# Two fused transformer blocks on one core: the opening of the program in another order

## What is computed

```
def rms_norm(x, g):
    y = x32 * lax.rsqrt(jnp.mean(jnp.square(x32), axis=-1, keepdims=True) + RMS_EPS)
    return (y * g.astype(jnp.float32)).astype(x.dtype)

u = rms_norm(h, g_mix[i])
z = u @ w_in[i]
q_a, k_a, v_a, q_b, k_b, v_b, f_b, gate_logits = jnp.split(z, SPLIT_POINTS, axis=-1)
y_a = sliding_window_attention(q_a, k_a, v_a, swa_sinks[i]) @ w_br_swa[i]
y_b = forgetting_attention(q_b, k_b, v_b, f_b + b_forget[i]) @ w_br_fox[i]
mixed = gates[:, :, 0] * y_a + gates[:, :, 1] * y_b
h = h + mixed @ w_mix_out[i]
```

## Time and profile before

| | us |
|---|---|
| median of 3 runs (lowest, highest) | 914.16 (913.61, 914.38) |
| span of the profiled execution | 912.5 |
| PE busy in it | 884.9 (97%) |
| DVE busy | 588.0 (64%) |
| ACT busy | 442.7 (49%) |
| POOL busy | 43.2 (5%) |
| mean DMA rate | 187 GB/s |

### The profile page before, as it was taken

The page is one execution under the profiler, slowest core; times in us unless marked ns, Lnnn a source line. Parts: engine busy times, 40 slices in busy tenths (PEclk is TensorE's granted clock), DMA queues, the critical chain, the costliest instruction groups (busy, mean ns, idle before and its releaser), DMA issues.

```text
span 912.5 us, 11670 instructions
## 1 busy us (share of the span) xinstructions
PE 884.9 (97%) x4071; PEld 712.6 (78%) x4071; DVE 588.0 (64%) x866; ACT 442.7 (49%) x694; POOL 43.2 (5%) x60
## 2 busy tenths in 40 slices
PE   6999999999999999999799999999999899999996
PEld 6787677787888888887687786778888778888885
DVE  4755544677777777788666795546667654654655
ACT  6545543446555555557553444444534443443442
POOL 1000000011000000020000000001000000000000
PEclk9999999999999999999899999999999899999999
DMA  9853332476999898751374445344545356565551
GB/s 290 285 174 116 93 93 79 136 274 225 353 329 326 321 319 328 246 162 37 120 226 145 156 147 188 93 139 152 176 157 184 108 172 192 161 217 187 165 157 47
DMA packets 87623, 170.43 MB, mean 187 GB/s; under 512 B 8177, under 2 KB 32985, under 8 KB 87585
## 3 DMA queue, kind: packets, MB, share of 16 engines
q1 hardware_dynamic: 82272, 142.63, 47.8%
q0 software_dynamic: 5312, 27.30, 8.7%
HBM read 168.84 MB, written 1.05 MB: 186 GB/s over the span
## 4 chain that ended last, share of the span: by engine, by line
PE 94%; DVE 2%; SPq 1%; ACT 1%; issue 1%; DMA 1%; POOL 0%; DVEq 0%; POOLq 0%; ACTq 0%
PE B L1418 27%; PE B L1420 26%; PE B L1419 26%; PE B L1458 3%; PE B L1562 2%; PE B L1480 2%; PE B L1702 1%; PE B L1753 1%; PE B L1469 1%; PE B L1739 1%; PE B L1481 1%; PE B L1823 1%; DMA raw<-in_w_in_dram 1%; DVE w_lo L891 1%; PE B L1564 1%
## 5 line engine op out<-in xcount | busy, mean ns | idle before, releaser
L1418 PE MATMUL B<-w_hi,xT_hi 128*128 128x512 f32 (+2 forms) x760 | 301.1, 396 | 1.3 <-DVE w_lo L891 1.3
L1420 PE MATMUL B<-w_hi,xT_lo 128*128 128x512 f32 (+2 forms) x760 | 294.6, 388 | 0.0
L1419 PE MATMUL B<-w_lo,xT_hi 128*128 128x512 f32 (+2 forms) x760 | 294.3, 387 | 0.0
L891 DVE TENSOR_TENSOR w_lo<-raw,w_hi 128x1024 fp32r<-128x1024 f32 (+2 forms) x156 | 186.9, 1210 | 90.8 <-ACT w_hi L520 89.3
L520 ACT ACTIVATE w_hi<-raw 128x1024 fp32r<-128x1024 f32 (+2 forms) x156 | 159.2, 1032 | 95.4 <-PE B L1420 88.6
L1418 PEld LDWEIGHTS B<-w_hi,xT_hi 128*128 128x128 f32 x760 | 144.4, 190 | 35.0 <-issue 6.6
L1420 PEld LDWEIGHTS B<-w_hi,xT_lo 128*128 128x128 f32 x760 | 144.2, 190 | 29.4
L1419 PEld LDWEIGHTS B<-w_lo,xT_hi 128*128 128x128 f32 x760 | 144.5, 190 | 26.7
L1418 PE MATMUL B<-w_hi,sT_hi 128*128 128x512 f32 x328 | 130.1, 397 | 0.0
L1420 PE MATMUL B<-w_hi,sT_lo 128*128 128x512 f32 x328 | 128.1, 391 | 0.0
L1419 PE MATMUL B<-w_lo,sT_hi 128*128 128x512 f32 x328 | 127.9, 390 | 0.0
(11 more groups left out here) (214 smaller groups left out, 717.8 us busy)
## 6 DMA issues: line engine op xcount, KB each, us to landing
raw<-in_w_in_dram SPq DMA_DIRECT2D x88, 512.0 KB, 3.5
raw<-in_w_ff_dram SPq DMA_DIRECT2D x64, 512.0 KB, 6.4
Z<-in_w_ada_dram POOLq DMA_DIRECT2D x32, 768.0 KB, 7.6
raw<-in_w_ffn_gate_dram SPq DMA_DIRECT2D x44, 256.0 KB, 3.3
raw<-in_w_ffn_up_dram SPq DMA_DIRECT2D x44, 256.0 KB, 4.0
raw<-in_w_ffn_down_dram SPq DMA_DIRECT2D x20, 512.0 KB, 4.3
raw<-in_w_mix_out_dram SPq DMA_DIRECT2D x8, 512.0 KB, 3.8
raw<-in_w_ple_gate_dram SPq DMA_DIRECT2D x8, 512.0 KB, 4.2
```

The costliest lines, as they stand in the source:

```text
L891: nc.vector.tensor_tensor(w_lo[:, u % SPLIT, :, 0:n], raw[:, st.slot[u], :, 0:n], w_hi[:, u % SPLIT, :, 0:n].bitcast(F32), ALU.subtract).t ...
L1418: nc.tensor.matmul(bank, xh, wh, start=start, stop=False)
L1419: nc.tensor.matmul(bank, xh, wl, start=False, stop=False)
L1420: return nc.tensor.matmul(bank, xl, wh, start=False, stop=stop)
```

## The change

Five edits, all in the first microseconds of the program.

- SP: between the two halves of x it loads units 0 and 1; after the second half come units 2 and 3 as before, then also units 4 and 5, and only then the table of constants and the vectors; units 6 and on follow.
- PE: it waits for the zeros that DVE writes at the start (`zeros`), runs 26 products of the zero tile with itself (`warm`, 128x128, into a bank whose content nobody reads), transposes g_mix, runs 10 more, transposes the first half of x, runs 12 more, multiplies units 0 and 1, transposes the second half of x, multiplies units 2 and 3.
- The transposed x goes to banks 2 to 5 in place of 0 to 3, so that chunk 0, which adds into banks 0 and 1, need not wait for both banks of a half.
- ACT and DVE: first half of x, units 0 and 1, second half of x, units 2 to 4, squares (ACT) and their sum (DVE), unit 5, then unit 6 behind `nr8`.
- The transposition of all vectors moves from behind chunk 0 to behind chunk 1, and ACT's copy of it moves with it.

```
@@ SP
             for half in range(2):
                 for t in range(TILES):
                     sp.dma_start(h[:, t, 512 * half:512 * half + 512], x[...]).then_inc(sem(f"x_in{half}"), 16)
-            for u in range(4):
+                for u in (2 * half, 2 * half + 1):
+                    load(u)
+            for u in (4, 5):
                 load(u)
...
-            for u in range(4, U_FFL):
+            for u in range(6, U_FFL):
                 load(u)
@@ ACT
-            wide_hi((0, 1), xT_hi, 0, V_GMIX)
-            split_to(0)
-            wide_hi((2, 3), xT_hi, 4, V_GMIX)
-            split_to(3)
+            wide_hi((2, 3), xT_hi, 0, V_GMIX)
+            split_to(1)
+            wide_hi((4, 5), xT_hi, 4, V_GMIX)
+            split_to(4)
             for half in range(2):
                 squares(0, half, None, 0)
+            split_to(5)
             act.wait_ge(sem("nr8_done"), 1)
             split_to(AHEAD + 3)
-            act.wait_ge(sem("vec_T"), 2)
-            nc.scalar.activation(vec[:, 8:], B[:, 7, 8:V_ROWS], ACT.Copy).then_inc(sem("vec_done"), 1)
@@ DVE
-            wide_lo((0, 1), xT_hi, xT_lo, 0, V_GMIX)
-            split_to(0)
-            wide_lo((2, 3), xT_hi, xT_lo, 4, V_GMIX)
-            split_to(3)
+            wide_lo((2, 3), xT_hi, xT_lo, 0, V_GMIX)
+            split_to(1)
+            wide_lo((4, 5), xT_hi, xT_lo, 4, V_GMIX)
+            split_to(4)
@@ PE
+            def warm(n):
+                for _ in range(n):
+                    nc.tensor.matmul(B[:, 6, 0:P], zero_r[:, :], zero_r[:, :], start=True, stop=True)
+            pe.wait_ge(sem("zeros"), 1)
+            warm(26)
...
+            warm(10)
             pe.wait_ge(sem("x_in0"), 32)
-            transposes((0, 1), lambda t, k: h[:, t, k * P:(k + 1) * P], "wt_done")
-            pe.wait_ge(sem("x_in1"), 32)
-            transposes((2, 3), lambda t, k: h[:, t, (4 + k) * P:(5 + k) * P], "wt_done")
+            transposes((2, 3), lambda t, k: h[:, t, k * P:(k + 1) * P], "wt_done")
+            warm(12)
...
                     if c == 0:
-                        pe.wait_ge(sem("wt_lo"), max(kp + 1, 2))
+                        if kp == 2:
+                            pe.wait_ge(sem("x_in1"), 32)
+                            transposes((4, 5), lambda t, k: h[:, t, (4 + k) * P:(5 + k) * P], "wt_done")
+                        pe.wait_ge(sem("wt_lo"), kp + 1)
...
-                if c == 0:
+                if c == 1:
                     pe.wait_ge(sem("vectors_in"), 112)
```

More of the change, by code:

```diff
@@ L622, in _ @@
                 if c == 1:
+                    act.wait_ge(sem("vec_T"), 2)
+                    nc.scalar.activation(vec[:, 8:], B[:, 7, 8:V_ROWS], ACT.Copy).then_inc(sem("vec_done"), 1)
                     act.wait_ge(sem("f_logit"), 1)
```

## The result

The changed kernel takes 920.48 us (median of 4 runs, 919.95 to 921.07), the kernel before beside it 914.02 us (913.61 to 914.38). The ratio is 1.0065 with an interval from 1.0049 to 1.0081: it is slower, by 4.5 to 7.4 us. The forecast was 923.4 within 917.8 to 925.2. The profiled execution grew from 912.5 to 919.0 us, by 6.5, where the sum said 9.2.

The account below looks back on a forecast made before the run. In the opening DVE's row from the squares to unit 7 was taken as the later clock, ahead of a closed PE stretch. 8.4 + 0.3 + 0.5 = +9.2 us gave a span of 921.7, a median of 923.4, range 917.8 to 925.2.

Parts of the forecast that it names:

- Steps 1 and 2: PE's opening: 26 zero products at 0.22 us, then g_mix and 10 more, delay x's first half from 5.77 to 9.4 us.
- Step 3: From x's first transposition to unit 0: unit 0 starts at 14.1 us in place of 11.24, the 12 zero products hidden.
- Step 4: Units 0 and 1 on PE: 24 products, clock rising between 17.5 and 20.2 us, ending at 18.5 to 19.4.
- T: The moment units 0 and 1 end on PE and the second half of x follows, taken as 19.1 us.
- Step 5: Second half of x behind unit 1: squares at T + 5.0, PE starts unit 7 at T + 18.6 = 37.7 us, 8.4 later.
- Step 6: Vectors transposed behind chunk 1, where nothing hides their transposition: +0.3 us.
- Step 7: Clock behind PE's new idle times: a fall costs between 0 and 1.7 us, taken as +0.5.
- likeliest case: The sum of the steps, +9.2 us, with ends from +7.9 (T = 18.5, no fall) to +10.9 us; 60%.
- A: Rival for the opening: zero products cost 0.11 us each by columns, clock still low; +5.9 us, 920.1 us; 12%.
- B: Rival for the opening: zero products lift the clock, unit 7 at 33.0 us; +4.4 us, 918.6 us; 16%.
- C: Rival joining A and B: x at 5.77 us at full speed, unit 7 at 30.9; 916.1 us; 4%.
- D: Rival: PE's later pauses, 10.5 us in all, swallow the delay, so not slower; 914.2 us or less; 8%.

Follow-up runs that it names:

- the later tables: The changed kernel with DVE's 24 small tables moved behind units 11 to 18, three behind each: 919.55 us, repeated at 917.91 us.
- the wide zero products: The kernel before with zero products of 512 columns, 6 ahead of g_mix, 2 ahead of each half of x, 2 behind the second: 913.95 us.
- 26 and 10 alone: The kernel before with only 26 zero products ahead of g_mix and 10 ahead of x: 917.16 us, ratio 1.0024.

## Why the prediction was right, and where its size was off

*What bounds.* Right. That unit 7 is released by DVE's row, and that the row begins at the squares, is what the later tables (pause gone, in two profiles), the wide zero products (level up, unit 7 unmoved) and the chain after show.

*Steps 1 and 2, zero products at 0.22 us.* Right: 5.81 us for 26, x at 9.35 for 9.4. The bound by columns, 0.11, is refuted at the lower level: 0.22 in all five profiles that have the 26. The floor that step 1 takes from the weight loads can be seen in the stretches. Where products have 72 columns, the loads of weights fill 5.00 of 5.00 us; with 264 columns 5.99 of 6.00 at the lower level and 2.40 of 2.40 at the full one; with 512, mostly, 146.84 of 192.00. One load takes 0.33 us at the lower level and 0.19 at the full one, and the loads start as far apart as the products:

```profile
12.04 0.33 PEld L1419 LDWEIGHTS B<-w_lo,xT_hi 128*128 128x128 f32 x1
12.26 0.33 PEld L1420 LDWEIGHTS B<-w_hi,xT_lo 128*128 128x128 f32 x1
...
457.33 0.19 PEld L1420 LDWEIGHTS B<-w_hi,xT_lo 128*128 128x128 f32 x1
457.44 0.19 PEld L1418 LDWEIGHTS B<-w_hi,xT_hi 128*128 128x128 f32 x1
```

In the change the loads of the 26 zero products take 5.62 us.

*Step 3.* Unit 0 at 13.90 for 14.1. Its last load piece landed at about 7.0 us, where the prediction had 8.8, and ACT wanted it at 12.0; the 12 zero products were hidden.

*Step 4.* T was 18.44 for 19.1. The level rose at 17.3, just under the lower bound of 17.5, and unit 0 was 0.2 earlier. The bounds themselves were too narrow: in the second profile the rise came at about 12.4 and T was 16.86, below the 18.5 at which the prediction let it end. That the profiled execution came so near to T is in part luck.

*Step 5.* From T to unit 7 it took 17.7 us for 18.6. The 0.9 lies ahead of the squares, T + 4.1 and not T + 5.0: I had taken the chain of the first half at the lower level with 0.2 off, but the transpositions ran wholly at the full one, and ACT began 0.64 us behind the first of them and not 1.22. The rest of it is that I added the lengths of ACT's rows, which overlap by a tenth where one follows another. The row behind was as priced: squares to nr8 4.3 us, nr8 to unit 7 9.3 for 9.2 to 9.4.

*Step 6.* 0.1 us for 0.3.

*Step 7* is the term that was mis-sized most, by 1.0 us. +0.5 was allowed for a fall of the clock in the new pauses. In this execution none came there, and one that the kernel before had was missing: at the pause near 225 us its transpositions took 1.97 us (granted clock 0.50 from 226 to 228 us), those of the change 1.09 (1.00 from 222 to 240 us).

```profile
225.53 1.97 PE L1458 MATMUL B<-cst,nat 128*128 128x128 f32 x8 [1.95 <-ACT nat L675]
```

```profile
232.56 1.09 PE L1460 MATMUL B<-cst,nat 128*128 128x128 f32 x8 [1.95 <-ACT nat L677]
```

So the term was -0.5. That PE can lose the full level in a pause is shown: seven of the fourteen profiles have a fall at this pause and seven have none. The sum of the misses is 1.5 (steps 4 and 5) + 0.2 + 1.0 = 2.7 us, the whole of 9.2 - 6.5. The ends that the prediction gives to its likeliest case are wrong by its own terms, too: T = 18.5 without a fall makes +8.1 and not +7.9, T = 19.4 with a whole fall +10.7 and not +10.9. The measured 6.5 lies below that case; it is in the stated range because the range also had to hold rivals A and B. The time alone would not have told these apart. The rows of the opening do.

*Rivals.* A is refuted by the 0.22. B, that zero products lift the clock, is refuted for the profiled execution and for the profile of 26 and 10 alone, but **not for all executions**: see below. C needs A's price and falls with it. D is refuted by the waits after 60 us.

## What to carry to other kernels

Before filling an engine's idle time, find which wait ends last where the closed stretch begins; here PE's slow products and a row of DVE ran side by side, and only the row counted. Filler in an engine's one stream delays whatever stands behind it, so its price has to be read at the clock level at which it runs (0.22 us here and not 0.11), and it has to end before the data lands (36 zero products moved x from 5.77 to 9.35 us, 18 left it at 5.67). Moving an input's preparation behind the first products puts everything that hangs on it later too, here the squares (19.71 for 13.29 us with this part alone); ask who else reads it before moving it. And take two profiles of each kernel before a difference of 1 or 2 us between two is put down to the edit.

## What the runs showed that I had not expected

**The level rose ahead of any real product, with narrow zero products and transpositions alone.** In the second profile of the changed kernel the rise is at about 12.4 us, ahead of any real product: the 12 zero products take 2.25 us where they took 2.80, and unit 0's first is 0.36 long where it was 0.56.

```profile
10.94 2.25 PE L1490 MATMUL B<-zero_r 128*128 128x128 f32 x12
13.90 0.36 PE L1420 MATMUL B<-w_hi,xT_hi 128*128 128x264 f32 x1 [0.71 <-DVE w_lo L893]
```

The profile of the repeated later tables shows the same, with 2.09 us for the 12. The 36 ahead of x, with next to nothing else on the engine for 8 us, brought no rise in the five profiles that have them: x's transpositions behind them ran at the lower level (1.93 us for 8 in four profiles, 3.63 for 16 in the fifth). PE had run the same stream in both executions of the changed kernel; the level differed, and no run shows why.

**What follows chunk 1 varies with the clock.** The span less the end of chunk 1 lies between 878.9 and 881.4 us over all fourteen profiles, with the same work of PE in it. The granted clock parts them without a remainder: seven have a fall between 223 and 235 us, in the pause of 1.95 us there or just behind it, and they take 880.4 to 881.4 us; the seven without it take 878.9 to 879.9. The means are 1.5 us apart, and that is an estimate of what one such fall costs. Whether the pause, the same in all, costs a fall differs from execution to execution.

This can account for medians of few runs that differ by 0.8 to 3 us where the opening differs by 2; it isn't shown, since only one execution of each has a profile. For effects of 1 us the opening's timeline says more than the time, but only between profiles in which the level rose at the same moment.
